# A two-block network on one core: the last softmax of the expert choice, row products of the gate phase, and two head norms move

## The reference, cut to what matters

```python
# block 1
o = attention(...)                            # [512, 1024], two parts of 512 columns
o = rms_norm(each part) * g_out               # "head norm 1": 2 groups
x = x + gate_m * (o @ w_out)                  # out projection, then routing and experts
# block 2
o = diff_attention(...)                       # 8 heads of 128 columns
o = rmsnorm(o, subln_g) * (1 - lam_init)      # "head norm 2": 8 groups
y_attn = o @ w_branch_attn
...
# expert choice, 8 heads, 2 lists of 128 keys, 16 best of each, 16 best of the 256 sums
s1, i1 = top_k(s[:, :, 0], 16); s2, i2 = top_k(s[:, :, 1], 16)
best, pos = top_k(s1[..., None] + s2[..., None, :], 16)
gate = softmax(best)
act = gelu(x @ u_tab[experts]) * gate
out = act @ v_tab[experts]
```

## Time and profile before

| what | value |
|---|---|
| median of the runs | 2869.01 us (2868.68 to 2870.0) |
| profiled execution: time, span | 2875.04 us, 2873.3 us |
| TensorE busy | 2652.2 us (92%) |
| VectorE, ScalarE, GpSimd busy | 63%, 37%, 33% |
| DMA | 646.25 MB, mean 225 GB/s |

### The profile page before, as it was taken

How to read it: one execution, slowest core, us unless ns; L and a number is a source line. 1 busy time by engine, 2 the same in 40 slices (tenths; PEclk the granted TensorE clock), 3 DMA queues, 4 the chain that set the end, 5 groups by cost and what they waited for, 6 DMA issues and landing times. The chain is left out here.

```text
span 2873.3 us, 36529 instructions
## 1 busy us (share of the span) xinstructions
PE 2652.2 (92%) x13817; PEld 2162.8 (75%) x13821; DVE 1810.5 (63%) x3192; ACT 1065.2 (37%) x1682; POOL 942.5 (33%) x476
## 2 busy tenths in 40 slices
PE   6997986989979999999897999999899989999999
PEld 4776773333367878878785899999899978888887
DVE  6958543111140627519844089898888967888888
ACT  3324632222232332137623224343555534333333
POOL 0011121222214331021042347887223243444442
PEclk9996997999969999989998999999999999999999
DMA  8830035999733445300222236786588899999995
GB/s 320 319 117 1 1 151 209 417 393 371 292 131 102 148 139 214 139 30 1 95 98 89 74 116 231 287 286 249 187 304 288 301 398 365 373 389 382 387 379 222
DMA packets 135610, 646.25 MB, mean 225 GB/s; under 512 B 21680, under 2 KB 22576, under 8 KB 91184
## 3 DMA queue, kind: packets, MB, share of 16 engines
q1 hardware_dynamic: 86512, 483.81, 44.8%
q0 software_dynamic: 48384, 158.38, 14.7%
q10 hardware_dynamic: 576, 2.27, 0.2%
HBM read 620.26 MB, written 75.50 MB: 242 GB/s over the span
## 5 line engine op out<-in xcount | busy, mean ns | idle before, releaser
L188 PE MATMUL psum<-h_hi,w_hi 128*128 128x384 f32 (+1 forms) x1808 | 667.7, 369 | 29.3 <-DVE h_lo L567 8.8
L190 PE MATMUL psum<-h_hi,w_lo 128*128 128x384 f32 (+1 forms) x1808 | 655.1, 362 | 0.0
L189 PE MATMUL psum<-h_lo,w_hi 128*128 128x384 f32 (+1 forms) x1808 | 654.3, 362 | 0.0
L169 POOL TENSOR_TENSOR w_lo<-ring,w_hi 128x2048 fp32r<-128x2048 f32 x46 | 215.0, 4673 | 754.0 <-ACT w_hi L162 713.7
L188 PEld LDWEIGHTS psum<-h_hi,w_hi 128*128 128x128 f32 x1808 | 343.9, 190 | 65.2 <-issue 26.0
L189 PEld LDWEIGHTS psum<-h_lo,w_hi 128*128 128x128 f32 x1808 | 344.1, 190 | 33.2 <-issue 1.9
L190 PEld LDWEIGHTS psum<-h_hi,w_lo 128*128 128x128 f32 x1808 | 343.2, 190 | 34.0
L2460 ACT ACTIVATE w_hi<-ring 128x2048 fp32r<-128x2048 f32 x127 | 242.5, 1909 | 219.8 <-PE psum L190 200.8
L188 PE MATMUL psum<-w_hi,a_hi 128*128 128x512 f32 x768 | 301.7, 393 | 11.5 <-DVE w_lo L2468 8.4
L190 PE MATMUL psum<-w_hi,a_lo 128*128 128x512 f32 x768 | 300.6, 391 | 0.0
L189 PE MATMUL psum<-w_lo,a_hi 128*128 128x512 f32 x768 | 300.5, 391 | 0.0
(11 more groups left out here) (484 smaller groups left out, 4595.6 us busy)
## 6 DMA issues: line engine op xcount, KB each, us to landing
ring<-in_weights SPq DMA_DIRECT2D x199, 1024.0 KB
w_expert_in<-in_experts_in SPq DMA_DIRECT2D x32, 2048.0 KB
hid_dram<-hid_acts SPq DMA_DIRECT2D x64, 384.0 KB
gates_dram<-block_gates SPq DMA_DIRECT2D x24, 1024.0 KB
hid_tiles<-hid_dram SPq DMA_DIRECT2D x64, 384.0 KB
gate_tiles<-gates_dram SPq DMA_DIRECT2D x15, 1536.0 KB, 12.4
o<-in_ada_later SPq DMA_DIRECT2D x16, 1024.0 KB, 6.3
w_expert_down<-in_experts_down SPq DMA_DIRECT2D x16, 1024.0 KB
```

The lines of the kernel that those rows point to most:

```text
L169: eng.tensor_tensor(lo, slot(k, n), hi.bitcast(F32), ALU.subtract).then_inc(k.w_ready, 1)
L188: k.nc.tensor.matmul(out, hi, x_hi, start=start, stop=False)
L189: k.nc.tensor.matmul(out, hi, x_lo, start=False, stop=False)
L190: return k.nc.tensor.matmul(out, lo, x_hi, start=False, stop=stop)
```

## The change

- `HeadNorm` replaces `head_norm_stage`: its parts for VectorE, TensorE and ScalarE are called at the start of the following stage's block, so there is one block less per norm, and `move_stage` goes too (its three loads are issued first in `mix_query_stage`). The four token tiles are scaled by two engines (norm 1: tiles 0, 1 by VectorE, 2, 3 by ScalarE; norm 2: 0, 1, 2 and 3), TensorE turns a tile as soon as it is scaled, into eight banks. `first_products` then does chunks 0 and 1 together, step by step as the low parts come. `before` is loaded after the rows of `k.o` have been read, behind the expert weights.
- Choice: `expo` is made ahead of the one-hot sums; the last tile's exponential is taken after batch 38, and its `finish` stands ahead of the last sum. Gathers are due three batches earlier, row products are paced over 33 steps instead of 36. The small table `ramp` becomes the 128-wide `iota`, which the tail stage then need not load.
- Gate phase: row products stand one by one after a hot row, `dots_within = (2, 2, 3, 3, 2, 2, 2, 2)` per batch in place of `(2, 2, 2, 2, 2, 2, 3, 3)`.

```diff
+def first_products(k, pe, outs, tile, source, done, ready):
+    wait_split(k, pe, tile)
+    hi, lo = parts(k, tile)
+    for kc in range(KC):
+        ready(min(kc + 1, KC - 1))
+        for c, out in enumerate(outs):
+            at = (c * KC + kc) * P
+            mm = split_products(k, out, hi[:, at:at + P], lo[:, at:at + P], source[0][:, kc], source[1][:, kc], kc == 0, kc == KC - 1)
+            if kc == KC - 1:
+                mm.then_inc(done, 1)
...
-def head_norm_stage(k, name, groups, gain, squares, gain_scale=1.0):
...
+class HeadNorm:
...
+        dve.wait_ge(rooted, turn + 1)
+        nc.vector.reciprocal(rstd[:], total[:]).then_inc(std_ready, 1)
+        dve.wait_ge(std_ready, 2 * turn + 2)
+        for t in self.by_vector:
+            rows = k.o[:, t].rearrange("p (g n) -> p g n", g=groups)
+            nc.vector.tensor_tensor(rows, rows, rstd[:, t].unsqueeze(2).broadcast_to([P, groups, width]), ALU.mult).then_inc(scaled[turn], 1)
+        for c in range(KC):
+            dve.wait_ge(k.activation_high, KC * self.high_turn + c + 1)
+            nc.vector.scalar_tensor_tensor(h_lo[:, c], k.psum[:, c], self.gains[:, c:c + 1], h_hi[:, c].bitcast(F32), ALU.mult,
+                                           ALU.subtract).then_inc(copied, 1)
...
+    def tensor(self, pe):
+        for t in self.order:
+            if t in self.by_vector:
+                pe.wait_ge(scaled[turn], self.by_vector.index(t) + 1)
+            else:
+                pe.wait_ge(scaled_by_scalar[turn], self.by_scalar.index(t) + 1)
+            for c in range(KC):
+                mm = nc.tensor.transpose(k.psum[:, c, t * P:(t + 1) * P], k.o[:, t, c * P:(c + 1) * P], k.ident[:])
+                if t == self.order[-1]:
                     mm.then_inc(turned, 1)
...
+    def scalar(self, act):
+        nc.scalar.activation(self.idle[:], k.eps[:, 0:1], ACT.Sqrt)
+        act.wait_ge(std_ready, 2 * turn + 1)
+        nc.scalar.activation(self.total[:], self.total[:], ACT.Sqrt).then_inc(rooted, 1)
+        act.wait_ge(std_ready, 2 * turn + 2)
+        for t in self.by_scalar:
+            for g in range(groups):
+                part = k.o[:, t, g * width:(g + 1) * width]
+                ins = nc.scalar.activation(part, part, ACT.Copy, scale=self.rstd[:, t, g:g + 1])
+            ins.then_inc(scaled_by_scalar[turn], 1)
+        for c in range(KC):
+            act.wait_ge(turned, KC * turn + c + 1)
+            nc.scalar.activation(self.parts[0][:, c], k.psum[:, c], ACT.Copy, scale=self.gains[:, c:c + 1]).then_inc(k.activation_high, 1)
...
+                norm.rows_read(sp)
+                sp.dma_start(before, k.d["before"]).then_inc(consts, 16)
                 stream(k, sp, first, COUNT["out1"])
...
-                chunk_products(k, pe, k.psum[:, 0], first, 0, (k.h_hi, k.h_lo), done)
+                norm.tensor(pe)
+                first_products(k, pe, [k.psum[:, c] for c in range(2)], first, (k.h_hi, k.h_lo), done, lambda kc: norm.split(pe, kc))
                 pe.wait_ge(scaled, 1)
                 pe.wait_ge(consts, earlier_consts + 96)
...
-                    due = 0 if b < 8 else 4 + (b - 8) * (EARLY_DOTS - 4) // (early_batches - 13)
+                    due = 0 if b < 8 else 4 + (b - 8) * (EARLY_DOTS - 4) // (early_batches - 16)
...
-                        while dots < min(EARLY_DOTS, (calls - 5) * EARLY_DOTS // 36):
+                        while dots < min(EARLY_DOTS, (calls - 5) * EARLY_DOTS // 33):
...
                     if t >= 1:
                         finish(t - 1)
+                        dve.wait_ge(ready, 3 * t)
+                    nc.vector.tensor_tensor(expo[:], best[:], best[:, :, 0:1].broadcast_to([P, H, K]), ALU.subtract).then_inc(ready, 1)
...
                         between(t)
+                        if t == TT - 1 and s == 1:
+                            finish(t)
-                        step(nc.vector.tensor_reduce(picked[:, s, t % 2], hot[:], AX.X, ALU.add))
+                        nc.vector.tensor_reduce(picked[:, s, t % 2], hot[:], AX.X, ALU.add).then_inc(ready if s == 1 else step.sem, 1)
...
-                    nc.vector.tensor_tensor(expo[:], best[:], best[:, :, 0:1].broadcast_to([P, H, K]), ALU.subtract).then_inc(ready, 1)
-                finish(TT - 1)
...
+                for b in range(SLOTS * last_loop, SLOTS * (last_loop + 1)):
+                    hidden_scalar(k, act, b, b)
+                    if b % SLOTS == SLOTS - 2:
+                        exp(TT - 1)
+                for t in range(TT - 2, TT):
+                    copy(t)
...
-    dots_behind = (2, 2, 2, 2, 2, 2, 3, 3)
+    dots_within = (2, 2, 3, 3, 2, 2, 2, 2)
...
-                    for blk, part, at in steps_behind(r) + (steps_within(r + 1) if r + 1 < body else []):
+                    started, due = g + r > 0, dots + dots_within[r]
+                    for i, (blk, part, at) in enumerate(steps_behind(r) + (steps_within(r + 1) if r + 1 < body else [])):
                         hot_rows(2 * steps * g + at)
+                        if (started or i > 0) and dots < due:
+                            row_dot(k, dve, dots, k.x_rows)
+                            dots += 1
```

More of the change, by code:

```diff
@@ L190, in split_products @@
     return k.nc.tensor.matmul(out, lo, x_hi, start=False, stop=stop)
-def split_stage(k, source):
-    nc = k.nc
-    high = k.activation_high
-    turn, k.activations = k.activations, k.activations + 1
-    with nc.Block(no_gpsimd_drain=True) as block:
-        @block.scalar
-        def _(act):
-            for c in range(KC):
-                nc.scalar.activation(k.h_hi[:, c], source[:, c], ACT.Copy).then_inc(high, 1)
-        @block.vector
-        def _(dve):
-            for c in range(KC):
-                dve.wait_ge(high, KC * turn + c + 1)
-                nc.vector.tensor_tensor(k.h_lo[:, c], source[:, c], k.h_hi[:, c].bitcast(F32), ALU.subtract)
 def stage_loads(k, count):
@@ L1003, in _ @@
                 sp.dma_start(b_route[:], k.d["b_route"][0].partition_broadcast(P)).then_inc(consts, 16)
-                for part, name in ((k.prio[:], "prio"), (before, "before"), (k.iota_row[:], "iota"), (k.token[:], "token")):
+                for part, name in ((k.prio[:], "prio"), (k.iota_row[:], "iota"), (k.token[:], "token")):
                     sp.dma_start(part, k.d[name]).then_inc(consts, 16)
@@ L1045, in _ @@
                 mm.then_inc(biased, 1)
-                for c in range(1, KC):
-                    if c >= 2:
-                        pe.wait_ge(added, c - 1)
+                pe.wait_ge(biased, 2)
+                logits(0)
+                for c in range(2, KC):
+                    pe.wait_ge(added, c - 1)
                     chunk_products(k, pe, k.psum[:, c % 2], first, c, (k.h_hi, k.h_lo), done)
-                    if c == 1:
-                        pe.wait_ge(biased, 2)
                     logits(c - 1)
@@ L2243, in mix_query_stage @@
     n = 2 * PEER_HEADS
+    k.moves += 3
     earlier_moves, moves = k.moves, k.moves + 1
@@ L2259, in mix_query_stage @@
     k.acts, k.pairs = late(tail, "hid_acts", [P, 2, 2, DENSE]), late(tail, "pairs", [P, 3, DENSE])
+    k.iota = late(tail, "iota", [P, P])
     k.rows, k.row_hid, k.row_gate = late(tail, "rows", [P, ROW_SLOTS, D]), late(tail, "row_hid", [P, PAIRS]), late(tail, "row_gate", [P, PAIRS])
@@ L2300, in stat @@
                 mm.then_inc(stat_done, 1)
-            for c in range(KC):
+            norm.tensor(pe)
+            first_products(k, pe, [k.psum[:, c] for c in range(2)], first, (branch_hi, branch_lo), branch_done.sem, lambda kc: norm.split(pe, kc))
+            for c in range(2, KC):
                 if c >= 4:
@@ L2357, in _ @@
         def _(dve):
+            norm.vector(dve)
             dve.wait_ge(k.moved, 16 * earlier_moves)
@@ L2413, in _ @@
         def _(act):
+            norm.scalar(act)
             for c in range(KC):
@@ L2753, in _ @@
                 turn(TT - 1)
-def move_stage(k, *moves, wait=True):
-    nc = k.nc
-    k.moves += len(moves)
-    with nc.Block(no_gpsimd_drain=True) as block:
-        @block.sync
-        def _(sp):
-            for to, source in moves:
-                sp.dma_start(to, source).then_inc(k.moved, 16)
-            if wait:
-                sp.wait_ge(k.moved, 16 * k.moves)
 def peer_tail_stage(k, tail):
@@ L2797, in peer_tail_stage @@
     flat = "p j t -> p (j t)"
-    iota = tail.enter_context(nc.sbuf_tensor("iota", [P, P], F32))
+    iota = k.iota
     with ExitStack() as scope:
@@ L2994, in _ @@
                         low(0, 0)
-                    for j in range(dots, dots + dots_behind[r]):
-                        row_dot(k, dve, j, k.x_rows)
+                    while dots < due:
+                        row_dot(k, dve, dots, k.x_rows)
                         dots += 1
@@ L3155, in build @@
         k.stage_loaded, k.stage_load_count = k.sem("stage_loaded"), 0
```

(4 more changed lines are left out.)

112 lines of the change are left out of this document (50 added, 62 removed).

## The result

The changed kernel takes 2852.7 us (median of 5 runs, 2849.3 to 2858.4) against 2868.7 of the kernel before on the same chip (2867.8 to 2870.0): a ratio of 0.9944, 95% interval 0.9931 to 0.9957. The forecast was 2847.2, in a range of 2838 to 2859. It is faster by 16.0 us, where 21.8 was forecast; the interval, 12 to 20 us, leaves the 21.8 out, though the time lies in the forecast's range. The profiled execution took 2852.7 us with a span of 2850.9.

A forecast was written before the change was run, and what follows sets the result against it. TensorE, with work for 92% of the span, was taken as the bound, plus its gaps. Gains of 5.1, 4.9, 2.5, 8.3 and 1.0 us sum to 21.8 off 2869.01, giving 2847.2 us, range 2838 to 2859.

The forecast's parts named there:

- A: First head norm: 5.1 us gained, from first product 4.4 earlier, 1.2 of clock regained, 0.5 lost; bounds 2.5 and 6.5.
- B: Second head norm: first product 5.8 us sooner, TensorE then waits 0.6 to 1; 4.9 us gained, bounds 2.5 and 6.5.
- C: End of the choice: VectorE's wait goes, but SP's last refill holds the block; 2.5 us gained, bounds 1 and 6.5.
- (d): Choice: GpSimd becomes the bound if a mean gather exceeds 1.5 us; at 2.2, 28 us slower, 2875; chance 0.04.
- D: Gate phase: two round boundaries lose 1.8 us each instead of 11.9 together; 8.3 us gained, bounds 3 and 11.9.
- E: After the third round: SP's load of hidden tile 2 comes earlier but DMA engines are full; 1 us, bounds 0 and 4.1.
- (a): Gate phase: rows still come late at a round's end; half the boundary gain, none at the end, 2852.4; chance 0.22.
- (b): More gained: boundaries lose nothing (3.6 more) or SP does not hold the choice's block (3.9 more), 2839.7 to 2843.6; chance 0.15.
- (c): Both norms: first products after the turns run at half speed, costing 1.2 and 1.7 us, 2850.1; chance 0.08.
- (e): No change: gathers in the choice at a mean of 1.9 us cancel most of the gain, 2863 to 2869; chance 0.06.

The follow-up runs named there:

- first-logits run: The changed kernel with the first chunk's logits of the first projection moved behind chunk 2: 2854.6 us, ratio 0.9942 to the kernel before.
- refill run: The changed kernel with SP's last weight-ring refill of the choice issued at the start of the gate phase: 2847.5 us, ratio 0.9921 to the kernel before.
- only the pace as before: The changed kernel with only the pacing of the choice's row products and gathers put back (36 places, 27 batches): 2848.9 us in one run.
- norms apart: The changed kernel with each head norm put back into its own block ahead of its projection: 2883.9 us, ratio 1.0040 to the kernel before.
- choice as before: The changed kernel with the choice's old order and pacing put back: 2858.8 us, ratio 0.9952 to the kernel before; once more, 2854.3 us in one run.
- first hot group earlier: The changed kernel with a round's first one-hot row group built in the previous round's last batch: 2853.9 us, ratio 0.9941 to the kernel before.
- all products behind: The changed kernel with the gate phase's new row-product counts kept but all products placed behind the hot rows: 2855.8 us in one run.

## Why the prediction was right, and where it was not

**A, first norm: 5.1 forecast, 3.5 measured.** The turns moved 3.4 us nearer to the start of scaling (4.69 to 1.28), the first product 4.1 (4.4 forecast). Both parts held up to chunk 2, which began 25.5 us after the block's start instead of 30.5: 5.0 us. The term that failed is the clock. The 1.2 us "regained" were regained, and 1.6 were lost again just behind (chunk 2 to route stage 44.0 instead of 42.4), since bias products, a short wait and logits now stand in a row between two chunks. The first-logits run moved the logits alone, and the loss was gone. `before` was hidden, but by less than forecast: counted from the start of scaling it was asked for after 20.4 us (20.1 forecast) and landed after 19.7, not 17.4, since more went ahead of it and more slowly (7.4 MB at 399 GB/s from 366 to 384.5, where 6.3 MB at 422 was counted). The spare 2.7 us were 0.7.

**B, second norm: 4.9 forecast, 5.5 measured.** The turns began 3.4 us after the block's start instead of 8.4, the first product 10.1 instead of 16.5. The 0.6 to 1 us that the joined chunks were to cost at chunk 4 is not to be seen as a wait; none over 0.3 us stands between the first product and the sums behind the projection. 0.9 us was given back behind the first product, 0.35 by those sums and 0.5 between them and the choice.

**C: 2.5 forecast, 2.4 measured**, and for the reason given. The refill run shows the other 4.1 us that SP kept. The pace of the gathers was priced at nothing, and gains nothing (347.0 without it); a batch stayed at about 8.35 us, with a mean gather of 1.33 us (1.29 over all 50) under the 1.5 from which rival (d) decides.

**D: 8.3 forecast, 4.5 measured** (4.1 at the boundaries, where 102.08 and 99.96 became 98.95 each, and 0.4 in the first batches, which vary by 1 us from run to run with the same code). The step that failed is "ready 2131.5, wanted 2130.1, 1.4 lost, and 0.4 in the batch after". The wait was 1.92, nearly that sum, but I counted only the wait. The gate products behind it ran at half the clock, 3.65 for 1.80. A boundary costs 3.85 and not 1.8: 1.9 of wait, 1.7 of clock (0.34 of 5 us at the window from 2115) and 0.2 more; 4.1 us over the two. The forecast took the kernel before's 7.0 and 4.9 as lateness of rows alone, while 3.4 of the 7.0 were clock; a look at that would have shown that a stall here can bring half speed with it. The product between the hot groups is the cause; with the new count alone the rounds were 97.1. Moving the hot rows one batch ahead took the stall and the half speed away together. A stall of 1.9 us does not always bring the half speed (last section), so the price of this step has a part that differs from run to run.

**E: 1.0 forecast, 0.8 measured.** SP's load was issued 3.1 us sooner behind the third round and landed 0.7 sooner: 16.6 us of flight instead of 14.2. Full DMA engines took the rest, as said.

**The rivals.** (a) is out: no landing in the chain, VectorE's waits for rows down to 5.7 from 24.7, though its price, half the boundary gain, is what came about by another way. (b) did not come, since SP holds the block; the refill run shows that the hold is real and can be taken away. (c) is out as told: the first products behind the turns ran at 1.00. The Trainium skill (TensorE: Matmul & The Clock Gate, Part 4: PE-mode transpose) says that the full clock doesn't engage for transposes, since they don't count as busy the same way; by that the first products would be slow. Neither norm agrees, with products of 0.39 us behind 6.33 and 5.15 us of turns, and the clock rose while TensorE did nothing but turns (second norm after, turns from 1412.98 to 1418.13):

```profile
1413.00:1416.00 3.00, 3.00 (x14) 3.00 (x15) 2.20 (x2) 1.15 (x4) 0.00 (x0) 0.50 0.98 415
1416.00:1419.00 3.00, 2.13 (x20) 1.89 (x18) 0.87 (x2) 1.59 (x3) 0.00 (x0) 1.00 0.98 421
```

That is stronger than the 0.97 that the forecast went by, a window in which TensorE stood idle for 2.3 of 5 us. In the first norm the half speed stood one stop later, behind narrow products. (d) and (e) did not come.

The total was nearer than its parts allow: B gave 0.6 more, A and D 1.6 and 3.8 less. That the time came out at rival (a)'s 2852.4 is luck, since its mechanism is not what happened. 16.7 from the stretches agrees with the 16.0 of the medians.

## What to carry to other kernels

When a stall shrinks but stays, price the products behind it at both levels of the clock, not the wait alone: here the half-speed stretch cost 1.7 us behind a wait of 1.92, and 1.6 behind one of 0.29. And read the kernel before for it: windows of the clock beside each stall tell which part of a loss is a wait. Where an engine's list is in order, move the work that a round's start needs into the last batch of the round before, rather than put other work between its pieces. And when a wait at a stage's edge goes, look at what SP's queue still has to issue there; joining two stages is worth more than its edge if loads are issued sooner by it. Before a difference of a few us is put down to an edit, compare the lengths of its gathers with those of the kernel it is compared with.

## What the runs showed of the hardware

- The same wait does not always have the same price. Seven profiles have the gate phase of the kernel after, with two boundaries each and 1.9 us of wait at every one. The 16 gate products behind it took 3.10 to 3.65 us in eight of the fourteen, 2.74 in one and 2.02 in five. In the run with only the pace as before, the round with 2.02 behind its wait took 97.7 us, the one with 2.74 took 98.9. What decides between the two stays open.
- A run of 36-column products with a 0.29 us wait in it was followed by 3.7 us at the lower clock (0.86 and 0.80 in two windows); without the logits in that run it was not (1.00 and 1.00).
- An indirect gather of 128 rows holds GpSimd for 1.2 us in the median, but in three of the fourteen profiles (norms apart, choice as before, first hot group earlier) some took 4 to 6 us, in each of the three a pair of 5.87 and 4.03; in the other eleven none took over 3.2. The rows landed late behind such a pair, and VectorE waited 2.4 to 3.2 us for them. Two of these three profiles are also the ones with 2.02 us at both boundaries. What makes the gathers slow stays open, as do the 2.60 us ahead of the combine's first product in the run with all products behind, which the profile puts down to issue alone.
- The stages ahead of the first norm and the MoE stage vary from run to run by 12 and 10 us, with the same code: the first turns of the first norm began at 362.88 in the pace run and at 375.30 in the choice run, and the MoE stage took 356.4 to 366.1 us. All other stretches repeat within about 3, but for the gate phase with slow gathers. That is where totals of one kernel get their spread; its cause stays open.
